# Products that need no corrected value, moved ahead of the waits in an RWKV-7 state phase

## The chip, the cores and the metric

The kernel runs on one core of a Trainium2 chip. The metric is the device time of one execution in microseconds. The core has five engines with a program each: PE (matrix products), DVE (vector), ACT (activation), POOL, and SP, which issues the DMAs. They meet only through semaphores. A product's result lies in one of eight PSUM banks until DVE or ACT has read it.

## The reference

A decoder trunk of two layers over 256 tokens of width 1024: an RWKV-7 time mix and a SwiGLU FFN, then dilated window attention and a second FFN. The change lies in the time mix, whose core is a recurrence of a 64 x 64 state for each of 16 heads, followed by a normalization of the output over each head:

```python
def step(state, inp):
    r_t, w_t, k_t, v_t, a_t, b_t = inp
    sa = jnp.einsum('bhij,bhj->bhi', state, a_t)
    state = (state * w_t[:, :, None, :] + sa[..., None] * b_t[:, :, None, :]
             + v_t[..., None] * k_t[:, :, None, :])
    return state, jnp.einsum('bhij,bhj->bhi', state, r_t)
...
o = wkv7_scan(rh, decay, kh, vh, -kk, kk * ah)
mean = jnp.mean(o, axis=-1, keepdims=True)
var = jnp.mean(jnp.square(o - mean), axis=-1, keepdims=True)
o = (o - mean) * lax.rsqrt(var + LNX_EPS)
```

## The kernel before

**Groups and chunks.** The time mix runs in four groups of 256 columns, that is four heads each (`it` 0 to 3), and each group in two chunks of 128 tokens. Within a chunk the recurrence is solved in closed form: masked products of scaled keys, receptances and values (the planes of `M`: 0 and 1 with the b vectors, 2 and 3 with the keys; 0 and 2 against a, 1 and 3 against r), a triangular inverse `Us` that is built over six levels, and from it the corrected values. The index `u` is a head of chunk 0 (0 to 3) or of chunk 1 (4 to 7).

**The tail of a group** (lines 805 to 849) is where the change lies. In the names of the code:

- `Zs`: what the values of earlier tokens and the carried state put on the a vectors. For chunk 0 there is no state; for chunk 1 it is `M` plane 2 by the values `Vn`, plus `ar` by the state `St` (bank 4, signalled as `pe_z1`).
- `UUs`: the corrected values, `Us` by `Zs` (banks 1 and 5, signalled as `pe_uu`, copied to SBUF by ACT, which signals `act_uu`).
- `St`: the state after chunk 0, keys by values (`kPn`, `Vn`) plus b by corrected values (`bPn`, `UUs`), in bank 2; DVE decays it and signals `dve_S`.
- The output of a chunk (banks 3 and 6, signalled as `pe_o`): `ar` by the state (chunk 1 only), `M` plane 3 by the values and `M` plane 1 by the corrected values.

**What stands between.** Each wait of PE on another engine in the tail is covered by `next_keys(v)`: in groups 0 to 2 a quarter of the next group's key projection, 12 products of 256 columns; in the last group, which has no successor, a few products of the identity with itself (`keep_clock`), whose result nobody reads.

**Behind the tail.** The output is normalized over each head (`norm_output`, lines 1645 to 1668, on DVE): sum, mean, centring (`dve_oc`), ACT's square (`square_output`), sum of squares (`dve_var`), POOL's inverse root, scaling (`dve_on`). Chunk 0 goes first, then chunk 1. On ACT the order is fixed by the program text (lines 1284 to 1296): copy of chunk 1's `Zs`, copy of chunk 1's corrected values, then, in groups 0 to 2, a sigmoid of one element, ahead of which a table load stands, then the square of chunk 0. In the next group PE projects three quarters of the receptances, transposes the normalized output (`turn_output`, line 596), sums the squares of the keys and goes on. In the last group ACT squares chunk 0 ahead of the two copies, and PE turns chunk 0's output between two waits of the tail, gates it (`gate_output` on DVE) and multiplies it by the output weights (`product_o`), then the same for chunk 1, which leads into the FFN.

All products of the tail are of fp32 operands; in the trace each such product stands as two records. The functions `mm` and `A` are helpers, so all products have line 496 and all of ACT's work line 1111.

Of the kernel before, what the change touches and what calls it, by code (L numbers as in the profile page):

```python
# [20 lines left out]
P = 128  # L21
D, T = 1024, 256
KT, RT = D // P, T // P
HD = 64
# [64 lines left out]
def program(nc, ins, out):  # L89
    ctx = ExitStack()  # L90
    with ctx:
# [3 lines left out]
        def sem(name):  # L95
            return ctx.enter_context(nc.semaphore(name))
# [59 lines left out]
        bank = [ctx.enter_context(nc.psum_tensor(f"bank{i}", [P, 512], F32)) for i in range(3)]  # L156
# [5 lines left out]
        bank = [b[:, :] for b in bank]  # L162
# [5 lines left out]
        def S(name):  # L168
            if name not in names:
                names[name] = sem(name)  # L170
            return names[name]
# [5 lines left out]
        M = work[:, 0:8 * 512].rearrange("p (u m t) -> p u m t", u=8, m=4)  # L177
# [18 lines left out]
        ar = cg.take(8 * P, "p (n c m t) -> p n c m t", n=2, c=2, m=2)  # L196
# [22 lines left out]
        Vn = spare_G.rearrange("p (c n i) -> p c n i", c=2, n=2)  # L219
        kPn, bPn = (spare_E[:, 256 * i:256 * i + 256].rearrange("p (n i) -> p n i", n=2) for i in range(2))  # L220
        Zs = cg.take(256)
        UUs = sa.rearrange("p n t -> p (n t)").rearrange("p (c n i) -> p c n i", c=2, n=2)
        St = cg.take(256, "p (n i) -> p n i", n=2)
# [270 lines left out]
        def _(pe):  # L494
            def mm(o, a, b, start=True, stop=True):
                return pe.matmul(o, a, b, start=start, stop=stop)  # L496

            def keep_clock(n, b):
                for _ in range(n):
                    mm(bank[b][:, 0:P], ident, ident)  # L500
# [25 lines left out]
            for k in range(KT):  # L526
                m = pe.transpose(bank[7][:, k * NR:(k + 1) * NR], rows[0:NR, k * P:(k + 1) * P], ident[0:NR, 0:NR])
            m.then_inc(S("pe_par"), 1)
            for r in range(RT):
                for j in range(2):  # L530
# [4 lines left out]
                    for q in range(4):  # L535
                        k = 4 * j + q
                        m = pe.transpose(bank[2 * r + j][:, q * P:(q + 1) * P], hn[:, r, k * P:(k + 1) * P], ident)
# [9 lines left out]
            for k in range(KT):  # L547
# [3 lines left out]
                if k % 4 == 3:  # L551
                    for s_ in range(4):
                        m = mm(bank[3 + s_][32 * s_:32 * s_ + 32, 0:T], g1s[:, k - 3 + s_, P:LG], xs[2][:, k - 3 + s_, :], k == 3, k == KT - 1)
# [26 lines left out]
            def project_parts(b, i, hi, parts, name, quarters=range(4)):  # L580

                w_parts = [v.rearrange("p (k n) -> p k n", k=KT) for v in (hi, mix_lo[:, i, :])]
                for n, k0 in ((v // 2, v % 2 * (KT // 2)) for v in quarters):
                    for k in range(k0, k0 + KT // 2):
                        for a, c in PASSES:
                            m = mm(bank[b][:, n * T:(n + 1) * T], w_parts[a][:, k, n * P:(n + 1) * P], parts[c][:, k, :],
                                   k == 0 and a + c == 0, k == KT - 1 and a == 1)
                if 3 in quarters:
                    m.then_inc(S(name), 1)
# [40 lines left out]
            def group(it, behind=True, ahead=True):  # L630


                def next_keys(v):
                    if ahead:
                        if v == 0:
                            pe.wait_ge(S("dve_x_lo"), 2)
                        if v < 2:
                            pe.wait_ge(S("dve_mix_lo"), it * 6 + v + 1)
                        project_parts(7, 1, kw_hi, (xk_hi, xk_lo), "pe_k", [v])
                    else:  # L640
                        keep_clock((4, 4, 4, 3)[v], 7)


                def sums_of_squares():
# [47 lines left out]
                for c in range(2):  # L692
# [5 lines left out]
                    for banks, src, read in ((MB, bP, 2), (MK, kP, 4)):  # L698
                        if c == 1:
                            pe.wait_ge(S("act_mats"), it * 8 + read)  # L700
                        for nn in range(2):
                            for h in range(2):
                                hp = slice(h * HD, (h + 1) * HD)
                                m = mm(bank[banks[h]][:, nn * 256:(nn + 1) * 256], src[hp, nn, c * P:(c + 1) * P],
                                       ar[hp, nn, c, :, :].rearrange("p m t -> p (m t)"))
# [47 lines left out]
                def quarter(b, u):  # L753
                    return b[:, u % 4 * QB:(u % 4 + 1) * QB]

                for l in range(1, LEVELS - 1):
                    corner = l == LEVELS - 2
                    for q in range(2):
# [3 lines left out]
                        for u in range(4 * q, 4 * q + 4):  # L762
                            for i, o in PAIRS if corner else zip(BLK, BLK):
                                w = corners[q][i, u % 4, o] if corner else M[i, u, 0, o]
                                m = mm(quarter(bank[q], u)[o, :], w, Tq[i, u, :])
# [6 lines left out]
                    for q in range(2):  # L772
                        pe.wait_ge(S("dve_X"), it * 12 + 2 * l + q - 1)
                        for u in range(4 * q, 4 * q + 4):
                            for o, i in PAIRS if corner else zip(BLK, BLK):
                                m = mm(quarter(bank[2 + q], u)[o, :], (Xq if corner else Xc)[i, u, :], Uc[i, u, :])
# [7 lines left out]
                for q in range(2):  # L784
                    pe.wait_ge(S("dve_U"), it * 12 + 11 + q)
                    for u in range(4 * q, 4 * q + 4):
                        m = pe.transpose(bank[4 + q][lo, u % 4 * HD:(u % 4 + 1) * HD], Us[lo, u, lo], ident[lo, lo])  # L787
                    m.then_inc(S("pe_T"), 1)
                next_keys(0)
                for q in range(2):  # L790
                    pe.wait_ge(S("act_T"), it * 2 + q + 1)
                    for u in range(4 * q, 4 * q + 4):
                        m = mm(bank[q][up, u % 4 * HD:(u % 4 + 1) * HD], corners[q][lo, u % 4, up], Tc[lo, u, :])
                    m.then_inc(S("pe_X"), 1)
                for q in range(2):
                    pe.wait_ge(S("dve_X"), it * 12 + 11 + q)
                    for u in range(4 * q, 4 * q + 4):
                        m = mm(bank[2 + q][lo, u % 4 * HD:(u % 4 + 1) * HD], Xc[up, u, :], Us[up, u, up])
                    m.then_inc(S("pe_U"), 1)

                def hcols(v, u):
                    return v[:, u * HD:(u + 1) * HD]
# [4 lines left out]
                for u in range(4):  # L807
                    m = mm(hcols(bank[1], u), Us[:, u, :], hcols(Zs, u))
                m.then_inc(S("pe_uu"), 1)
                next_keys(1)  # L810
                pe.wait_ge(S("act_uu"), it * 2 + 1)
                for n in range(2):
                    mm(bank[2][:, n * P:(n + 1) * P], kPn[:, n, :], Vn[:, 0, n, :], True, False)
                    m = mm(bank[2][:, n * P:(n + 1) * P], bPn[:, n, :], UUs[:, 0, n, :], False, True)
                m.then_inc(S("pe_S"), 1)
                for u in range(4):
                    hh = slice((u % 2) * HD, (u % 2 + 1) * HD)
                    mm(hcols(bank[3], u), M[:, u, 3, :], Vn[:, 0, u // 2, hh], True, False)
                    m = mm(hcols(bank[3], u), M[:, u, 1, :], UUs[:, 0, u // 2, hh], False, True)
                m.then_inc(S("pe_o"), 1)  # L820

                pe.wait_ge(S("dve_S"), it + 1)
                pe.wait_ge(S("pool_M"), it * 2 + 2)
                for n in range(2):
                    mm(bank[4][:, n * P:(n + 1) * P], ar[:, n, 1, 0, :], St[:, n, :], True, False)
                    for h in range(2):
                        u = 2 * n + h
                        m = mm(hcols(bank[4], u), M[:, 4 + u, 2, :], Vn[:, 1, n, h * HD:(h + 1) * HD], False, h == 1)
                m.then_inc(S("pe_z1"), 1)
                next_keys(2)  # L830
                pe.wait_ge(S("act_z"), it * 2 + 2)
                pe.wait_ge(S("act_U"), it * 2 + 2)
                for u in range(4):
                    m = mm(hcols(bank[5], u), Us[:, 4 + u, :], hcols(Zs, u))
# [2 lines left out]
                if not ahead:  # L837
                    turn_output(NGRP, [0])
                pe.wait_ge(S("act_uu"), it * 2 + 2)
                for n in range(2):  # L840
                    mm(bank[6][:, n * P:(n + 1) * P], ar[:, n, 1, 1, :], St[:, n, :], True, False)
                    for h in range(2):
                        u = 2 * n + h
                        hh = slice(h * HD, (h + 1) * HD)
                        o = hcols(bank[6], u)
                        mm(o, M[:, 4 + u, 3, :], Vn[:, 1, n, hh], False, False)
                        m = mm(o, M[:, 4 + u, 1, :], UUs[:, 1, n, hh], False, h == 1)
                m.then_inc(S("pe_o"), 1)


# [7 lines left out]
            project(7, 1, xk, "pe_k", (1, 2, 3))  # L858
            pe.wait_ge(s_const, 16)
            group(0, behind=False)  # L860
            for it in range(1, NGRP):
                group(it, ahead=it < NGRP - 1)
# [1334 lines left out]
```

## Time and profile before

| | |
|---|---|
| median of 3 runs | 928.52 us (928.47 to 928.74) |
| profiled execution | 934.33 us |
| span of its instructions | 932.0 us |
| mean granted clock of TensorE | 0.993 |
| PE busy / DVE / ACT / POOL | 920.8 / 681.7 / 501.8 / 101.4 us |

The four groups of the time mix lie in the span's first 263 us. The tail of group 0 runs from 75.6 to 88.0 us, those of groups 1 and 2 from 133.6 to 146.0 and from 190.8 to 203.2, that of the last group from 249.3 to 262.8. Times are from the start of the span. The granted clock is a share of 2.4 GHz.

### The profile page before, as it was taken

How to read it: one execution, taken by the hardware profiler on the slowest of the kernel's cores; microseconds unless marked ns; L12 is line 12 of the kernel's file. 1: busy time of each engine (PE TensorE's matmuls, PEld its weight loads, DVE VectorE, ACT ScalarE, POOL GpSimd, SP SyncE). 2: the span in 40 equal slices, each digit the busy share in tenths (PEclk: the TensorE clock that was granted, in tenths of full speed). 3: DMA queues.
4: the chain of work that ended last, by engine and by line, in shares of the span. 5: the costliest groups of instructions: out<-in, count | busy, mean ns of one | idle time of the engine just before them, and what ended most of it. 6: DMA issues, size and time to landing. Idle time of an engine off the chain costs nothing.

```text
span 932.0 us, 18317 instructions
## 1 busy us (share of the span) xinstructions
PE 920.8 (99%) x7008; PEld 818.6 (88%) x7008; DVE 681.7 (73%) x1294; ACT 501.8 (54%) x818; POOL 101.4 (11%) x75
## 2 busy tenths in 40 slices
PE   9999999999999999999999999999999999999998
PEld 7789889798879888888899999999998888888887
DVE  7877877778466756666687888889879666666665
ACT  4563544544244545444457776767777445445442
POOL 0211000000012000000041133213222000000000
PEclk9999999999799999999999999999999999999999
DMA  9311213203407676667369545554654256676661
GB/s 298 132 60 46 91 60 105 92 1 107 145 1 202 178 223 178 185 193 217 104 206 292 152 132 163 148 155 139 171 159 114 71 162 186 192 203 195 188 180 45
DMA packets 195241, 136.71 MB, mean 147 GB/s; under 512 B 7390, under 2 KB 186078, under 8 KB 195180
## 3 DMA queue, kind: packets, MB, share of 16 engines
q1 hardware_dynamic: 194748, 135.13, 49.3%
q8 instruction: 44, 0.72, 0.3%
q10 hardware_dynamic: 432, 0.72, 0.3%
q14 instruction: 17, 0.14, 0.1%
HBM read 134.78 MB, written 1.05 MB: 146 GB/s over the span
## 4 chain that ended last, share of the span: by engine, by line
PE 94%; DVE 3%; issue 2%; ACT 1%; POOL 0%; POOLq 0%; DVEq 0%
PE bank L496 52%; PE wide L496 37%; DVE work L1505 1%; PE wide L1029 1%; PE wide L1052 1%; PE bank L1029 1%; PE bank L1052 1%; DVE x L1505 0%; POOL gsm L2123 0%; PE wide L653 0%; PE wide L741 0%; PE wide L787 0%; PE bank L519 0%; ACT work L1111 0%; PE bank L596 0%
## 5 line engine op out<-in xcount | busy, mean ns | idle before, releaser
L496 PE MATMUL bank<-wpj,hkq 128*128 128x384 f32 x1152 | 215.5, 340 | 1.5 <-ACT Vs L1111 0.4
L496 PEld LDWEIGHTS bank<-wpj,hkq 128*128 128x128 f32 x1152 | 197.5, 188 | 6.1 <-issue 4.2
L496 PE MATMUL wide<-hsp,wsp 128*128 128x256 f32 (+2 forms) x1120 | 196.0, 329 | 1.6 <-DVE hsp L1505 1.6
L496 PEld LDWEIGHTS wide<-hsp,wsp 128*128 128x128 f32 x1120 | 172.4, 190 | 24.3 <-DVE hsp L1505 2.4
L1505 DVE TENSOR_TENSOR wsp<-ring,wsp 128x1024 fp32r<-128x1024 f32 (+1 forms) x88 | 150.6, 1752 | 4.2 <-ACT wsp L1111 4.2
L1111 ACT ACTIVATE wsp<-ring 128x1024 fp32r<-128x1024 f32 (+1 forms) x88 | 130.3, 1484 | 26.5 <-DMA ring<-in_f_w_gu 15.6
L2123 POOL TENSOR_TENSOR gsm<-gsm,mhalf 128x6 f32<-128x6 f32 (+1 forms) x40 | 74.3, 1876 | 317.4 <-DVE gsm L2041 174.0
L1111 ACT ACTIVATE rows<-wide 128x256 f32<-128x256 f32 x66 | 25.4, 384 | 145.7 <-PE wide L496 145.7
L496 PE MATMUL bank<-wsp,asp 128*128 128x512 f32 x396 | 98.1, 392 | 0.0
L1505 DVE TENSOR_TENSOR wpj<-ring,wpj 128x1536 fp32r<-128x1536 f32 x48 | 84.1, 1753 | 17.0 <-ACT wpj L1111 17.0
L496 PEld LDWEIGHTS bank<-wsp,asp 128*128 128x128 f32 x396 | 71.8, 189 | 13.1
L1111 ACT ACTIVATE wpj<-ring 128x1536 fp32r<-128x1536 f32 x48 | 71.1, 1485 | 6.6 <-PE bank L496 6.3
L496 PEld LDWEIGHTS bank<-work 64*64 64x64 f32 (+4 forms) x1216 | 58.9, 140 | 16.1 <-issue 6.2
L496 PE MATMUL bank<-work 64*64 64x32 f32 (+7 forms) x1216 | 71.1, 237 | 1.6
L1505 DVE TENSOR_TENSOR am<-sg,rows 128x256 f32<-128x256 f32 x44 | 19.1, 435 | 71.4 <-ACT sg L1111 70.8
L496 PE MATMUL bank<-hsp,wsp 128*128 128x256 f32 (+1 forms) x368 | 68.7, 330 | 0.0
L1111 ACT ACTIVATE work<-wide 128x256 f32<-128x256 f32 (+3 forms) x73 | 30.9, 441 | 67.6 <-PE wide L496 28.6
L496 PE MATMUL wide<-work 64*64 64x32 f32 (+6 forms) x720 | 62.7, 265 | 0.7 <-DVE work L1505 0.4
L496 PEld LDWEIGHTS bank<-hsp,wsp 128*128 128x128 f32 x368 | 56.9, 190 | 6.2
L496 PEld LDWEIGHTS wide<-work 64*64 64x64 f32 (+4 forms) x720 | 54.4, 160 | 4.5 <-issue 1.7
L1505 DVE TENSOR_TENSOR rows<-wide,rows 128x256 f32<-128x256 f32 x66 | 27.9, 424 | 37.3 <-ACT rows L1111 37.3
L496 PE MATMUL wide<-wsp,asp 128*128 128x512 f32 x132 | 37.1, 390 | 0.0
(295 smaller groups left out, 1333.4 us busy)
## 6 DMA issues: line engine op xcount, KB each, us to landing
ring<-in_f_w_gu SPq DMA_DIRECT2D x88, 512.0 KB, 6.0
ring<-in_w_kv SPq DMA_DIRECT2D x96, 256.0 KB, 3.5
ring<-in_f_w_down SPq DMA_DIRECT2D x44, 512.0 KB, 3.7
ring<-in_b_w_q SPq DMA_DIRECT2D x48, 256.0 KB, 3.4
wmix<-in_a_w_k SPq DMA_DIRECT2D x4, 1024.0 KB, 5.2
wmix<-in_a_w_r SPq DMA_DIRECT2D x4, 1024.0 KB, 5.6
wmix<-in_a_w_v SPq DMA_DIRECT2D x4, 1024.0 KB, 5.3
wmix<-in_a_w_o SPq DMA_DIRECT2D x4, 1024.0 KB, 5.0
```

Of the source, the lines that this page charges most:

```text
L496: return pe.matmul(o, a, b, start=start, stop=stop)
L1029: m = pe.transpose(QK[w][r][:, g * P:(g + 1) * P], akr[:, 2 * w + r, g * P:(g + 1) * P], ident)
L1052: m = pe.transpose(SCORES[r][h][:, j * P:(j + 1) * P], pr[r][:, h, j * P:(j + 1) * P], ident)
L1111: return act.activation(o, i, f, **k)
L1505: return dve.tensor_tensor(o, a, b, op)
L2123: return pool.tensor_tensor(dst, src, mhalf[:, 0:n], ALU.pow)
```

## The change

Only PE's program is edited. Four moves and a subtraction:

- Chunk 0's keys by values go from behind the wait for chunk 0's corrected values to a place ahead of it (ahead of `next_keys(1)`).
- Chunk 1's plane 2 by values go from behind the wait for the state to a place ahead of it; the wait for POOL's masks moves with them.
- Chunk 1's `ar` by state and plane 3 by values, which open its output, go from behind the wait for chunk 1's corrected values to a place right behind `pe_z1`, ahead of `next_keys(2)`.
- A bank's first product alone opens the accumulation and its last alone closes it.
- In the last group `keep_clock` does 4, 2, 3 and 3 products, not 4, 4, 4 and 3.

```diff
-                        keep_clock((4, 4, 4, 3)[v], 7)
+                        keep_clock((4, 2, 3, 3)[v], 7)
...
                 m.then_inc(S("pe_uu"), 1)
+                for n in range(2):
+                    mm(bank[2][:, n * P:(n + 1) * P], kPn[:, n, :], Vn[:, 0, n, :], n == 0, False)
                 next_keys(1)
                 pe.wait_ge(S("act_uu"), it * 2 + 1)
                 for n in range(2):
-                    mm(bank[2][:, n * P:(n + 1) * P], kPn[:, n, :], Vn[:, 0, n, :], True, False)
-                    m = mm(bank[2][:, n * P:(n + 1) * P], bPn[:, n, :], UUs[:, 0, n, :], False, True)
+                    m = mm(bank[2][:, n * P:(n + 1) * P], bPn[:, n, :], UUs[:, 0, n, :], False, n == 1)
                 m.then_inc(S("pe_S"), 1)
...
                 m.then_inc(S("pe_o"), 1)
+                pe.wait_ge(S("pool_M"), it * 2 + 2)
+                for u in range(4):
+                    mm(hcols(bank[4], u), M[:, 4 + u, 2, :], Vn[:, 1, u // 2, u % 2 * HD:(u % 2 + 1) * HD], u == 0, False)
 
                 pe.wait_ge(S("dve_S"), it + 1)
-                pe.wait_ge(S("pool_M"), it * 2 + 2)
                 for n in range(2):
-                    mm(bank[4][:, n * P:(n + 1) * P], ar[:, n, 1, 0, :], St[:, n, :], True, False)
-                    for h in range(2):
-                        u = 2 * n + h
-                        m = mm(hcols(bank[4], u), M[:, 4 + u, 2, :], Vn[:, 1, n, h * HD:(h + 1) * HD], False, h == 1)
+                    m = mm(bank[4][:, n * P:(n + 1) * P], ar[:, n, 1, 0, :], St[:, n, :], False, n == 1)
                 m.then_inc(S("pe_z1"), 1)
+                for n in range(2):
+                    mm(bank[6][:, n * P:(n + 1) * P], ar[:, n, 1, 1, :], St[:, n, :], n == 0, False)
+                for u in range(4):
+                    mm(hcols(bank[6], u), M[:, 4 + u, 3, :], Vn[:, 1, u // 2, u % 2 * HD:(u % 2 + 1) * HD], False, False)
                 next_keys(2)
...
                 pe.wait_ge(S("act_uu"), it * 2 + 2)
-                for n in range(2):
-                    mm(bank[6][:, n * P:(n + 1) * P], ar[:, n, 1, 1, :], St[:, n, :], True, False)
-                    for h in range(2):
-                        u = 2 * n + h
-                        hh = slice(h * HD, (h + 1) * HD)
-                        o = hcols(bank[6], u)
-                        mm(o, M[:, 4 + u, 3, :], Vn[:, 1, n, hh], False, False)
-                        m = mm(o, M[:, 4 + u, 1, :], UUs[:, 1, n, hh], False, h == 1)
+                for u in range(4):
+                    m = mm(hcols(bank[6], u), M[:, 4 + u, 1, :], UUs[:, 1, u // 2, u % 2 * HD:(u % 2 + 1) * HD], False, u == 3)
                 m.then_inc(S("pe_o"), 1)
```

What this does to PE's order is shown at two places. `wide` holds banks 3 and 4, `wide2` banks 5 and 6; the size behind an operation is partitions by columns of the moving operand. First group 0 (groups 1 and 2 read alike), from the wait for chunk 0's corrected values to the third quarter of the key projection. Before:

```order
L496 MATMUL bank2<-work 128x128 [waits act_uu]
L496 MATMUL bank2<-work 128x128 x3
L496 MATMUL wide<-work 128x64 x8
L496 MATMUL wide<-work 128x128 [waits pool_M,dve_S]
L496 MATMUL wide<-work 128x64 x2
L496 MATMUL wide<-work 128x128
L496 MATMUL wide<-work 128x64 x2
L496 MATMUL bank7<-x_hi,w_hi 128x256
```

And changed, the same stretch:

```order
L496 MATMUL bank2<-work 128x128 [waits act_uu]
L496 MATMUL bank2<-work 128x128
L496 MATMUL wide<-work 128x64 x8
L496 MATMUL wide<-work 128x64 [waits pool_M]
L496 MATMUL wide<-work 128x64 x3
L496 MATMUL wide<-work 128x128 [waits dve_S]
L496 MATMUL wide<-work 128x128
L496 MATMUL wide2<-work 128x128 x2
L496 MATMUL wide2<-work 128x64 x4
L496 MATMUL bank7<-x_hi,w_hi 128x256
```

Two keys-by-values products have left the top of the stretch, and the six products into `wide2` that open chunk 1's output now stand ahead of the key projection, which itself stands ahead of the corrected values of chunk 1.

Second the last group, from the wait for the state to the output of chunk 1 (`bank7<-cst` are the fillings, line 596 turns chunk 0's output). Before:

```order
L496 MATMUL wide<-work 128x128 [waits pool_M,dve_S]
L496 MATMUL wide<-work 128x64 x2
L496 MATMUL wide<-work 128x128
L496 MATMUL wide<-work 128x64 x2
L496 MATMUL bank7<-cst 128x128 x4
L496 MATMUL wide2<-work 128x64 [waits act_U,act_z]
L496 MATMUL wide2<-work 128x64 x3
L496 MATMUL bank7<-cst 128x128 x3
L596 MATMUL bank2<-cst,work 128x128 [waits dve_on]
L596 MATMUL bank2<-cst,work 128x128
L496 MATMUL wide2<-work 128x128 [waits act_uu]
L496 MATMUL wide2<-work 128x64 x4
```

And changed:

```order
L496 MATMUL wide<-work 128x128 [waits dve_S]
L496 MATMUL wide<-work 128x128
L496 MATMUL wide2<-work 128x128 x2
L496 MATMUL wide2<-work 128x64 x4
L496 MATMUL bank7<-cst 128x128 x3
L496 MATMUL wide2<-work 128x64 [waits act_U,act_z]
L496 MATMUL wide2<-work 128x64 x3
L496 MATMUL bank7<-cst 128x128 x3
L596 MATMUL bank2<-cst,work 128x128 [waits dve_on]
L596 MATMUL bank2<-cst,work 128x128
L496 MATMUL wide2<-work 128x64 [waits act_uu]
L496 MATMUL wide2<-work 128x64 x3
```

The six products into `wide2` moved up past the third fillings (one fewer), the corrected values, the fourth fillings and the transposes; of chunk 1's output only the four products by the corrected values stay behind the last wait.

## Rows read from the trace of the kernel before

**Rows 1.** The page, busy time of each engine: us (share), instructions.

```profile
PE 920.8 (99%) x7008; PEld 818.6 (88%) x7008; DVE 681.7 (73%) x1294; ACT 501.8 (54%) x818; POOL 101.4 (11%) x75
```

**Rows 2.** Chain of waits, 80 to 108 us: start, us, what.

```profile
83.59 0.85 PE wide L496 x8
...
84.46 0.39 ACT work L1111
...
84.87 1.28 ACT L1111
...
87.41 1.93 POOL gsm L2123
...
94.04 0.66 PE bank L596 x4
```

**Rows 3.** Timeline of PE, 72 to 100 us: start, us, operation [idle before].

```profile
83.43 1.00 PE L496 MATMUL wide<-work 128*128 128x64 f32 x8
84.23 0.37 PE L496 MATMUL bank<-x_hi,w_hi 128*128 128x256 f32 x1
...
85.73 2.34 PE L496 MATMUL wide<-work 128*128 128x128 f32 x20
88.00 1.14 PE L496 MATMUL bank<-work,wa 64*128 64x256 f32 x8
...
94.04 0.66 PE L596 MATMUL bank<-cst,work 128*128 128x128 f32 x4 [0.44 <-DVE work L1505]
```

**Rows 4.** Timeline of ACT, 72 to 100 us.

```profile
84.46 0.39 ACT L1111 ACTIVATE work<-wide 128x256 f32<-128x256 f32 x1 [1.92 <-PE wide L496]
```

**Rows 5.** Timeline of DVE, 72 to 100 us.

```profile
81.48 0.42 DVE L1505 TENSOR_TENSOR work<-wide,gsm 128x256 f32<-128x256 f32 x1
...
84.09 2.35 DVE L1505 TENSOR_TENSOR wmix_low<-wmix,vw_hi 128x1024 fp32r<-128x1024 f32 x2
...
93.59 0.39 DVE L1505 TENSOR_TENSOR work<-work,gsm 128x256 f32<-128x256 f32 x1
```

**Rows 6.** Timelines of PE and DVE at the second and third turn.

```profile
151.41 0.60 PE L596 MATMUL bank<-cst,work 128*128 128x128 f32 x4
...
150.66 0.39 DVE L1505 TENSOR_TENSOR work<-work,gsm 128x256 f32<-128x256 f32 x1
...
208.68 0.60 PE L596 MATMUL bank<-cst,work 128*128 128x128 f32 x4
...
207.93 0.39 DVE L1505 TENSOR_TENSOR work<-work,gsm 128x256 f32<-128x256 f32 x1
```

**Rows 7.** Timeline of PE and its weight loads (PEld), last group's tail.

```profile
251.03 2.02 PE L496 MATMUL bank<-cst 128*128 128x128 f32 x8
...
257.63 1.11 PE L496 MATMUL bank<-cst 128*128 128x128 f32 x8
258.58 1.00 PE L496 MATMUL wide<-work 128*128 128x64 f32 x8
...
260.29 0.20 PEld L596 LDWEIGHTS bank<-cst,work 128*128 128x128 f32 x2 [0.18 <-DVE work L1505]
...
262.75 3.65 PE L496 MATMUL bank<-wmix,work 128*128 128x512 f32 x8
```

**Rows 8.** Timeline of DVE in the last group's tail, 248 to 274 us.

```profile
261.41 0.42 DVE L1505 TENSOR_TENSOR work<-work 128x256 f32<-128x256 f32 x1
262.95 0.42 DVE L1653 TENSOR_REDUCE gsm<-wide 128x4 f32<-128x256 f32 x1 [1.11 <-PE wide L496]
```

**Rows 9.** Engines' busy time by stretch; PEclk is the granted clock's share.

```profile
70.30:73.60 3.30, 3.30 (x20) 3.08 (x20) 1.23 (x2) 0.28 (x2) 0.00 (x0) 0.50 0.00 0
240.00:244.00 4.00, 3.88 (x99) 3.37 (x95) 3.31 (x12) 2.59 (x7) 0.00 (x0) 1.00 0.03 10
244.40:254.50 10.10, 10.10 (x63) 9.76 (x63) 3.15 (x3) 1.26 (x4) 0.00 (x0) 0.50 0.26 74
...
249.30:254.50 5.20, 5.20 (x25) 5.20 (x25) 1.20 (x1) 0.76 (x2) 0.00 (x0) 0.50 0.50 144
```

## The prediction

> **What bounds the kernel now.** The page comes first: PE is busy 99% of the span [rows 1]. That share alone would say that only fewer PE instructions help. So the chain of waits is read next, round the end of the first column group, where the edit lies. There the chain leaves PE at 84.44, passes through ACT, DVE and POOL, and comes back at 94.04 with four transposes [rows 2]; in between PE works on other things, so it looks busy, but it isn't what is waited for. The timelines of the engines say what that detour is. The eight PE records at 83.43 are the corrected values of chunk 1 (four products; an fp32 product leaves two records) [rows 3]. ACT copies them at 84.46, having been idle 1.92 us for them [rows 4], and everything behind that copy on ACT is in program order: the table load (84.87, 1.28 us), the one-element sigmoid, and the square of chunk 0's centred output. DVE had that output centred from 81.48 on, 0.42 us long [rows 5], so the square could have begun some 2.5 us before the copy; it doesn't, because it stands behind it. From the square on: sum, POOL's root (87.41), the scaling, then the same for chunk 1, and at 93.59 DVE writes the scaled output that the transposes need. PE has no work left and idles 0.44 us ahead of them [rows 3]. At the second turn (group 1 to 2) and the third (2 to 3) the same write begins at 150.66 and 207.93, and PE comes to its transposes at 151.41 and 208.68 without a wait [rows 6].
>
> In these three tails PE waits for nothing: products follow at the spacing of back-to-back records from 83.43 through 88.00 [rows 3], because projections of the next group's keys stand in every wait. The last group has no next keys; there identity products fill, and PE (its weight load) waits once, 0.18 us, at 260.29 [rows 7].
>
> **The change, part by part.**
>
> *Groups 0 to 2.* The same products are issued, so PE's end of the tail doesn't move, unless a wait goes; there is none to take. What moves is the order. Four records (keys by values) go ahead of the key projection; PE reaches the state products no sooner, since the total ahead of them is equal: nothing. Eight records (values through the mask, chunk 1) go ahead of the wait for the state: nothing either, for the same reason. Twelve records of the chunk 1 output (4 of 128 columns, 8 of 64) move from behind the last wait to a place ahead of the third key projection, and so ahead of the corrected values of chunk 1. Those come later by the price of twelve records. Twenty such records start at 85.73 and the next work at 88.00 [rows 3]: 2.27 us, 0.1135 each, so 12 x 0.1135 = 1.36 us. The bounds: by the eight narrow ones at 83.43, 0.80 us to the next row [rows 3], 12 x 0.100 = 1.20; and as the twenty less eight narrow ones, 2.27 - 0.80 = 1.47.
>
> The copy on ACT, then the table load, the square and the whole detour move by this 1.36 us; no step of it has another input that comes later (DVE's low parts of the weights end at 84.09 + 2.35 = 86.44 [rows 5], ahead of the sum even now). At the first turn there is no slack, since PE waits already: +1.36. At the other two the write ends at 150.66 + 0.39 = 151.05 and 207.93 + 0.39 = 208.32; the hand-over takes 0.06 (93.59 + 0.39 = 93.98 to 94.04), so PE could have gone 0.30 earlier each time [rows 3, 5, 6]. 1.36 - 0.30 = +1.06 each. Sum: 1.36 + 1.06 + 1.06 = +3.48. Behind the transposes on PE stand the sums of squares of the keys, and for them wait ACT's root, the scaled keys and the triangular solve; nothing there has a source that doesn't move along, so I let all of it reach the end. The key weights that SP loads when the projection is done (chunk after chunk, used a group later) start 1.36 us later and are hidden by a whole solve.
>
> *The last group.* Here records are removed: two fillings in the wait for chunk 0's corrected values and one in the wait for chunk 1's state part, six records. Eight such cost 258.58 - 257.63 = 0.95 [rows 7], so 6 x 0.119 = 0.71. (The first two stand at half clock, where they cost nearly double, 2.02 us busy for eight at 251.03 against 1.11 for eight at 257.63 [rows 7]; but PE is busy throughout, and if the clock comes back at the same moment as now, what is saved ahead of it is that much work at full clock.) The 0.18 us wait at 260.29 also goes, since the twelve records now stand ahead of it: PE would be through with the chunk 1 output 0.89 earlier. Two things hold it. The transposes of chunk 0 were reached at 260.29 - 0.18 = 260.11; now 260.11 - 0.71 + 1.36 = 260.76, 0.47 later than they ran. DVE's gating behind them, which ended at 261.41 + 0.42 = 261.83, ends at 262.30, and the output product starts at 262.36 and not at 262.75 [rows 7, 8]: -0.39. DVE, which must finish that gating first, then begins the sums of chunk 1 at 262.30 and not at 262.95 [rows 8]: -0.65. This second chain decides, as the sums lead to the root, the next transposes and the FFN's input. I take -0.65, with -0.39 and -0.89 as bounds.
>
> **The sum**: 3.48 - 0.65 = +2.83 us. It is made on the profiled execution, which took 934.33 us (span 932.0 and 2.33 around it), 5.81 more than the median of 928.52. Applied to the median: 931.35, so **931.4**. Bounds of the terms alone: 1.20 + 0.90 + 0.90 - 0.89 = +2.1 and 1.47 + 1.17 + 1.17 - 0.39 = +3.4, so 930.6 to 931.9; as the slack at the second and third turn may be some tenths more in an execution without a profile, 930.4 to 931.9.
>
> **Rivals.**
>
> *The delay is hidden; not slower.* The 5.81 us by which the profiled execution is longer may lie in the detours of many small instructions, so that without a profile the scaled output is ready earlier against PE. Where it is ready 1.36 us ahead at each turn, nothing is lost and the last group's gain stands: 928.52 - 0.65 = 927.9. For it: I can't see where the 5.81 lies. Against it: at the first turn PE waits 0.44 now, and the detour would have to shrink by 1.8 of 9.6 us.
>
> *The half clock goes; not slower.* From 244.4 to 254.5 PE ran at the lower of its two levels (0.50, 1.2 GHz), and also from 70.3 to 73.6; the longer stretch began after 4 us in which PE was busy 3.88 us, with 99 small records [rows 9]. The change shifts the later groups by 1 to 3 us and could move them off the moment at which the clock falls. In 249.3 to 254.5, 25 records took 5.20 us, 0.208 each [rows 9], against 0.119 for a filling at full clock: 25 x 0.089 = 2.2 us is the least that a recovered stretch gives; half of 10.1, that is 5.0, the most. Middle 3.6: 931.4 - 3.6 = 927.8.
>
> *Another stretch at half clock; slower still.* The same shift could make the clock fall in group 1 or 2, where it now holds. A short stretch (3.3 us) costs at most 1.65, a long one the 3.6 above: 933.0 to 935.0. The Trainium skill (TensorE: Matmul & The Clock Gate, Part 1) ties the lower clock to an idle engine. The trace differs, as the busy 3.88 of 4 us just given show; by the page neither of these two rivals would have a chance, and the forecast would stand as it is.
>
> *The early products are cheap; not slower by a measurable amount.* If a 64-column record cost half of a 128-column one (0.119 from the fillings [rows 7]), twelve would take 4 x 0.119 + 8 x 0.059 = 0.95, the turns 0.95 + 0.65 + 0.65, and the sum would be +1.6: 930.1. Against it stands that eight narrow records took 0.80 us and eight wide fillings 0.95 [rows 3, 7]. The Trainium skill (the same page, Back-to-back issue gap) goes further: 60 cycles for up to 64 columns and 134 for 128. By that the twelve would take an estimated 0.42 us, and the whole change about nothing, 928.5. Its section on loading weights, by which the time goes with the 128 columns of the weights, agrees with the rows instead.
>
> **Chances.** Forecast 0.60; hidden 0.12; half clock gone 0.10; another half-clock stretch 0.13; cheap products 0.05. A change of 0.2% (1.9 us, about what a measurement of this kernel can tell from none) begins at 930.4 and 926.7. Slower: the forecast less 0.01 at its lower edge, and the further stretch, 0.72. Faster: the most favourable part of the recovered clock (a gain of 5.0 gives 926.4), 0.04. Same: 0.24. The range reaches from the hidden case to a short further stretch, 927.7 to 933.0; the likeliest case's own is 930.4 to 931.9.
>
> **What would show it.** In groups 0 to 2 of the changed kernel ACT's copy of the corrected values of chunk 1 should start some 1.36 us later, with a longer idle time ahead of it (1.92 becomes about 3.3), and PE should wait about 1.8, 1.06 and 1.06 us ahead of the transposes at the three turns. In the last group the output product should start about 0.4 and the second transposes about 0.65 us earlier, counted from the first corrected values. The granted clock should fall in the same two places. The forecast is wrong if PE doesn't wait at the second and third turn, or if the clock's stretches change in number.

## The result, and the profile after

| | before | changed |
|---|---|---|
| median of 10 | 929.07 us (928.47 to 931.48) | 933.22 us (931.28 to 936.72) |
| ratio, 95% interval | | 1.0042 [1.003, 1.0055] |
| profiled execution | 934.33 us, span 932.0 | 934.60 us, span 932.3 |

The change makes the kernel slower by 0.42%, 3.9 us. The ten times of the changed kernel fall in two parts by their mean granted clock: five executions at 1.000 take 931.28 to 932.18 us, five at 0.995 or 0.996 take 934.26 to 936.72. The median, 933.22, is the middle between the two parts; no execution lies there. The profiled one belongs to the second part. The profiled execution of before had a clock of 0.993; other executions of that kernel at 1.000 have spans of 925.8 us and up. So the two spans, 932.0 and 932.3, must not be compared as they stand; stages are compared instead.

Chain of waits of the changed kernel, 82 to 97 us, the lines that answer to [rows 2]:

```profile
83.89 0.85 PE wide L496 x8
...
84.76 0.38 ACT work L1109
...
85.16 1.28 ACT L1109
...
87.71 1.93 POOL gsm L2121
...
94.35 0.66 PE bank L596 x4
```

It is the same detour as before, from the corrected values of chunk 1 through ACT's copy to the transposes, and of the same length: 83.89 to 94.35 is 10.46, 83.59 to 94.04 was 10.45. What has changed is where it starts. PE's timeline round it, 75 to 100 us (answers to [rows 3]):

```profile
77.82 4.58 PE L496 MATMUL wide<-work 128*128 128x64 f32 x40
...
83.72 1.00 PE L496 MATMUL wide<-work 128*128 128x64 f32 x8
...
86.05 1.00 PE L496 MATMUL wide<-work 128*128 128x64 f32 x8
86.98 1.13 PE L496 MATMUL bank<-work,wa 64*128 64x256 f32 x8
...
94.35 0.66 PE L596 MATMUL bank<-cst,work 128*128 128x128 f32 x4 [1.77 <-DVE work L1503]
```

Of the 40 records at 77.82 the last twelve open chunk 1's output; behind the corrected values (83.72) only eight are left for it (86.05). From the corrected values to the next group's first product, PE needed 88.00 - 83.43 = 4.57 us and now needs 86.98 - 83.72 = 3.26: it gets there 1.31 us sooner after the corrected values, while the detour takes as long as ever. So it waits 1.77 us at the transposes where it waited 0.44. ACT's timeline shows the other side of it (answers to [rows 4]):

```profile
84.76 0.38 ACT L1109 ACTIVATE work<-wide 128x256 f32<-128x256 f32 x1 [3.23 <-PE wide L496]
```

The copy of chunk 1's corrected values now follows 3.23 us of idleness, not 1.92. PE at the second and third turn (answers to [rows 6]):

```profile
155.55 0.66 PE L596 MATMUL bank<-cst,work 128*128 128x128 f32 x4 [0.86 <-DVE work L1503]
...
213.88 0.66 PE L596 MATMUL bank<-cst,work 128*128 128x128 f32 x4 [0.87 <-DVE work L1503]
```

Before, neither of these turns had a wait [rows 6]. The last group (PE answers to [rows 7]):

```profile
259.53 0.89 PE L496 MATMUL bank<-cst 128*128 128x128 f32 x6
260.25 1.00 PE L496 MATMUL wide<-work 128*128 128x64 f32 x8
261.09 0.89 PE L496 MATMUL bank<-cst 128*128 128x128 f32 x6
261.81 0.38 PE L596 MATMUL bank<-cst,work 128*128 128x128 f32 x2
262.03 1.00 PE L496 MATMUL wide<-work 128*128 128x64 f32 x8
263.36 3.70 PE L496 MATMUL bank<-wmix,work 128*128 128x512 f32 x8 [0.32 <-DVE work L1503]
```

No wait is left ahead of the transposes of chunk 0 (261.81), and the output product (263.36) now waits 0.32 us for DVE's gating of chunk 0, as the prediction had it. The engines' busy time by stretch, with the granted clock as PEclk (answers to [rows 9]):

```profile
92.50:94.30 1.80, 0.08 (x1) 0.00 (x0) 1.72 (x6) 1.80 (x7) 1.02 (x1) 1.00 0.00 0
95.10:101.90 6.80, 6.80 (x33) 6.80 (x33) 4.44 (x11) 4.20 (x7) 0.00 (x0) 0.50 0.21 68
102.00:110.00 8.00, 8.00 (x62) 7.15 (x61) 6.20 (x12) 1.98 (x5) 0.00 (x0) 1.00 0.49 160
```

PE is busy 0.08 of the 1.80 us ahead of the transposes, and from 95.1 to 101.9 it runs at the lower level (1.2 GHz), on projections whose records come at 0.21 us each. In this execution the stretches of before at 70 and 244 us are absent. So the clock's stretches changed in number, from two to one, which the prediction had named as a sign of being wrong.

### The profile page after: what moved, and what is told of

It reads as the page before. It is cut to its first block, busy times and chain, and to the rows that moved or that the text cites. A ratio compares the mean times of both kernels' runs of the same rounds, so it can differ in the third digit from the quotient of the medians.

```text
span 932.3 us, 18301 instructions
## 1 busy us (share of the span) xinstructions
PE 917.8 (98%) x7002; PEld 815.4 (87%) x7002; DVE 681.4 (73%) x1294; ACT 501.3 (54%) x818; POOL 101.2 (11%) x75
## 3 DMA queue, kind: packets, MB, share of 16 engines
HBM read 134.78 MB, written 1.05 MB: 146 GB/s over the span
## 4 chain that ended last, share of the span: by engine, by line
PE 92%; DVE 4%; issue 2%; ACT 1%; POOL 0%; POOLq 0%; DVEq 0%
PE bank L496 51%; PE wide L496 37%; DVE work L1503 2%; PE bank L1050 1%; PE wide L1027 1%; PE bank L1027 1%; PE wide L1050 1%; ACT work L1109 0%; DVE work L1698 0%; POOL gsm L2121 0%; ACT L1109 0%; DVE x L1503 0%; PE wide L741 0%; PE wide L653 0%; PE wide L787 0%
## 5 line engine op out<-in xcount | busy, mean ns | idle before, releaser
L496 PE MATMUL bank<-work 64*64 64x32 f32 (+7 forms) x1216 | 68.3, 233 | 1.8
L496 PEld LDWEIGHTS bank<-work 64*64 64x64 f32 (+4 forms) x1216 | 55.8, 135 | 16.2 <-issue 5.9
```

## The experiments

Two theories were on record for the delay. **A**: it runs through ACT's order, the late copy holding up the table load and the square of chunk 0. **B**: the products cost more where they stand now. For the executions at a lower clock there were **C**, the wait at the first turn lets the clock fall, and **D**, the shift of the groups does.

**square_first** (the changed kernel, ACT's order edited):

```diff
-                    if c == 1 and not ahead:
-                        square_output(NGRP, 0)
+                    if c == 1:
+                        square_output(it + 1, 0)
...
                     A(small[:, 63:64], onec[:, 0:1], ACT.Sigmoid)
-                    square_output(it + 1, 0)
```

> The changed kernel, but in groups 0 to 2 ACT squares chunk 0's centred output ahead of the two copies of chunk 1, as it does in the last group already. PE's program is that of the change. Theory A (the delay runs through ACT's order: late copy, then table load and square): chunk 0's normalization no longer hangs on the corrected values of chunk 1, so the extra waits at the three turns go, PE waits under 0.4 us ahead of the transposes at the first turn and not at the others, and only the last group's gain is left: 927.3 to 928.2 us at full clock. Theory B (the products themselves cost more where they stand now, or open the accumulation at a price): nothing moves, 931.3 at full clock as the changed kernel.

Measured: 927.74 us, ratio to before 0.9979 [0.9966, 0.9992]; none of 12 executions is under a clock of 0.998. ACT's timeline at the first turn:

```profile
80.22 0.42 ACT L1109 ACTIVATE work<-work 128x256 f32<-128x256 f32 x1 [2.89 <-DVE work L1502]
80.55 0.37 ACT L1109 ACTIVATE work<-wide 128x256 f32<-128x256 f32 x1
84.09 0.39 ACT L1109 ACTIVATE work<-wide 128x256 f32<-128x256 f32 x1 [3.18 <-PE wide L496]
```

And PE's:

```profile
83.06 1.00 PE L496 MATMUL wide<-work 128*128 128x64 f32 x8
85.36 1.00 PE L496 MATMUL wide<-work 128*128 128x64 f32 x8
...
91.98 0.65 PE L596 MATMUL bank<-cst,work 128*128 128x128 f32 x4
```

The square (80.22) now precedes the copy of the corrected values by 3.9 us. That copy is as late as in the changed kernel (idle 3.18 us ahead of it). PE's program is unedited, and its row at the transposes shows no wait. Theory A holds, B falls: the products cost no more where they stand now than where they stood.

**open_late_in_013** (the six products wait again for the last corrected values in groups 0, 1 and 2, label notwithstanding; in the last group, which isn't `ahead`, they stay early):

```diff
-                for n in range(2):
-                    mm(bank[6][:, n * P:(n + 1) * P], ar[:, n, 1, 1, :], St[:, n, :], n == 0, False)
-                for u in range(4):
-                    mm(hcols(bank[6], u), M[:, 4 + u, 3, :], Vn[:, 1, u // 2, u % 2 * HD:(u % 2 + 1) * HD], False, False)
+                def open_output():
+                    for n in range(2):
+                        mm(bank[6][:, n * P:(n + 1) * P], ar[:, n, 1, 1, :], St[:, n, :], n == 0, False)
+                    for u in range(4):
+                        mm(hcols(bank[6], u), M[:, 4 + u, 3, :], Vn[:, 1, u // 2, u % 2 * HD:(u % 2 + 1) * HD], False, False)
+
+                if not ahead:
+                    open_output()
                 next_keys(2)
...
                 pe.wait_ge(S("act_uu"), it * 2 + 2)
+                if ahead:
+                    open_output()
```

> The changed kernel, but the six products that open chunk 1's output stand ahead of the third key projection in the last group alone; in groups 0 to 2 they are back behind the wait for the corrected values. Theory A: ACT's copy of the corrected values comes at the time of before (idle 1.9 us ahead of it), no waits at the second and third turn, 0.4 at the first, and the last group keeps its 0.65: 927.9 us at full clock. If the last group gains nothing: 928.5. Theory B (the moves of keys by values and of plane 2 cost as well): over 929.

Measured: 928.38 us, ratio 0.999 [0.9977, 1.0004]; the median of its six executions at clock 1.000 is 927.84, that of 23 of before beside it 929.15. PE at the three turns:

```profile
93.20 0.66 PE L596 MATMUL bank<-cst,work 128*128 128x128 f32 x4 [0.44 <-DVE work L1509]
...
150.50 0.60 PE L596 MATMUL bank<-cst,work 128*128 128x128 f32 x4
...
207.68 0.60 PE L596 MATMUL bank<-cst,work 128*128 128x128 f32 x4
...
260.81 0.38 PE L596 MATMUL wide<-cst,work 128*128 128x128 f32 x2
```

The first turn's wait is that of before to the hundredth, the others are gone. From the third turn to the transposes of chunk 1 (207.68 to 260.81) it takes 53.13 us.

**open_late_all** (the third move undone in all groups; the first two and the three fillings given up stay: the six products follow `pe.wait_ge(S("act_uu"), it * 2 + 2)` everywhere).

> The changed kernel with the third move undone in all four groups; the first two moves and the three fillings given up stay. Theory A: turns as before, and the last group gains only by the first two fillings, since its wait for chunk 0's scaled output is still there: 928.5 - 0.44 = 928.1 us at full clock. Theory B: the first two moves cost part of the 2.8, over 929.

Measured: 928.52 us, ratio 0.9986 [0.997, 1.0003]. PE's rows:

```profile
92.48 0.65 PE L596 MATMUL bank<-cst,work 128*128 128x128 f32 x4 [0.45 <-DVE work L1503]
...
207.03 0.60 PE L596 MATMUL bank<-cst,work 128*128 128x128 f32 x4
```

Counted from the first record of chunk 0's corrected values to the transposes, the three turns take 18.45, 17.83 and 17.84 us, and 18.45, 17.84 and 17.85 in before: the first two moves cost nothing there. The time itself can't tell a gain of 0.4 us from none.

**open_early_alone** (the kernel before with the third move alone; the six products stand behind `pe_z1` and leave the last wait, as in the change's diff).

> The kernel before with the third move alone (the six products that open chunk 1's output, in all four groups); the first two moves aren't made and the fillings are 4, 4, 4 and 3. Theory A: the turns cost 1.36 + 1.05 + 1.03 = 3.44, and the last group gains nothing, as chunk 0's gating comes 1.2 us later and DVE begins the sums of chunk 1 at the same time (+0.07): 932.0 us at full clock, more where the clock falls in the wait at the first turn. Theory B: 928.5 to 929.

Measured: 935.31 us, ratio 1.0068 [1.0049, 1.0087]. One execution of six is at 1.000 (931.94), five at 0.995 or 0.996 (934.87 to 937.14). PE:

```profile
93.81 0.66 PE L596 MATMUL bank<-cst,work 128*128 128x128 f32 x4 [1.78 <-DVE work L1503]
...
152.16 0.66 PE L596 MATMUL bank<-cst,work 128*128 128x128 f32 x4 [0.89 <-DVE work L1503]
...
210.55 0.66 PE L596 MATMUL bank<-cst,work 128*128 128x128 f32 x4 [0.89 <-DVE work L1503]
```

The third move by itself makes all three waits of the changed kernel. Its loss at full clock rests on that one execution: 931.94, where 932.0 was expected, is 2.8 above the 929.15 of before beside it.

**open_late_in_0** (as open_late_in_013, with `it > 0` for `not ahead` and `it == 0` for `ahead`).

> The changed kernel with the third move undone in group 0 alone. Theory A, with a price for each turn of its own: the first turn's 1.36 us is given back, the second and third keep 1.05 and 1.03, the last group its gain: 931.35 - 1.36 = 930.0 us at full clock. Theory C: PE waits 0.44 us at the first turn as before, and no execution falls to half clock there. If the delay of one turn were swallowed by the next: 931.3 or 927.9.

Measured: 931.48 us, ratio 1.0024 [1.0014, 1.0033]; four executions of 11 at 1.000, median 930.38, lowest 929.71, and before beside it 928.72 and 928.04. PE waits 0.44, 0.86 and 0.88 us at the three turns. The loss at full clock, 1.66 to 1.67, is nearer to 1.05 + 1.03 - 0.65 = 1.43 than to 2.8 or to a gain: the turns add up singly, none swallows another's delay. The profiled execution is at 1.000; where the clock fell in the seven below it (0.994 to 0.999) isn't known. Of the 31 of before beside it 14 are below 1.000 too, so this run says little on C.

**square_first_on_before** (ACT's edit on the kernel before) and **both_repairs** (ACT's edit and open_late_in_013).

> The kernel before with ACT's square of chunk 0 ahead of the copies of chunk 1, and nothing else. Theory A: at the first turn the chain then waits for DVE's low parts of the weights and not for the square, 0.25 us sooner; at the second and third PE didn't wait: 928.5 - 0.25 = 928.25 us. If square_first owes its gain to ACT's order alone and not to the last group: 927.5.

> Third move in the last group alone, and ACT squares chunk 0 ahead of the copies of chunk 1 in all groups. Theory A: the square moved ahead already hides the delay of the third move, so taking that move back in groups 0 to 2 adds nothing: the same as square_first within 0.3 us, 927.3 to 927.6 at full clock. If part of the delay was still there in square_first, up to 1 us less.

Measured: 928.25 us, 0.9991 [0.9979, 1.0003], and 928.77 us, 0.9994 [0.9985, 1.0003]. At 1.000 their medians are 928.01 (of 7) and 927.56 (of 5). Neither is told from before by its interval; the order at full clock is the expected one, and both_repairs isn't better than square_first (927.63 of 10, on another chip). square_first_on_before has the last group of before at full clock, which the first profile lacked: from the third turn to the transposes of chunk 1 it takes 262.70 - 208.94 = 53.76 us. Its PE rows from the third turn on:

```profile
208.94 0.60 PE L596 MATMUL bank<-cst,work 128*128 128x128 f32 x4
...
247.76 1.08 PE L496 MATMUL bank<-work 128*128 128x64 f32 x8
...
258.70 3.65 PE L496 MATMUL bank<-wmix,work 128*128 128x512 f32 x8
...
262.70 0.44 PE L596 MATMUL wide<-cst,work 128*128 128x128 f32 x2
```

Against 53.13 in open_late_in_013 that is a gain of 0.63 for the last group; open_late_all, with the fillings alone, takes 260.40 - 207.03 = 53.37, a gain of 0.39. The same shows in the changed kernel itself, counted from the first corrected values as the prediction asked (rows of the changed kernel):

```profile
252.81 1.58 PE L496 MATMUL bank<-work 128*128 128x64 f32 x12
...
267.12 0.38 PE L596 MATMUL wide<-cst,work 128*128 128x128 f32 x2
```

To the output product (263.36) it takes 10.55 us, and 258.70 - 247.76 = 10.94 in square_first_on_before: 0.39 earlier. To the second transposes it takes 14.31, and 262.70 - 247.76 = 14.94 there: 0.63 earlier.

**fill_the_turns**, **changed_again** and **fill_first_turn** are for the clock. The first and third are the changed kernel with identity products ahead of the transposes at the turns (7, 3 and 3, and 7 at the first alone); the second is the changed kernel itself beside the third.

```diff
                     project_parts(4, 0, rw_hi, (xr_hi, xr_lo), "pe_r", (0, 1, 2))
+                    keep_clock((0, 7, 0, 0)[it], 5)
                     turn_output(it)
```

> The changed kernel, with identity products ahead of the transposes at the turns: 7 at the first, 3 each at the second and third, so that PE works where it now waits. They lie inside the waits (7 x 2 records x 0.117 = 1.64 of 1.77 us; 0.70 of 0.86), so at full clock nothing is lost: 931.3 to 931.6. Theory C (the clock falls because of the wait of 1.77 us at the first turn): no execution has the half-clock stretch behind the first turn that the changed kernel's profile shows at 95 us, and the times near 934.4 are gone. Theory D (it falls by the shift of the solves against the moments at which the clock can change): executions near 934.4 remain in a like share, 5 of 10.

> The changed kernel unaltered, beside the next one on the same chip. If the wait of 1.77 us at the first turn is what lets the clock fall (theory C), about half of the executions have a mean granted clock of 0.995 or 0.996 and take some 934.5 us, the others 931.3 to 932.2 at 1.000, as in the first ten.

> The changed kernel with 7 identity products ahead of the transposes at the first turn alone. Theory C: no execution at 0.995 or 0.996; those without a fall elsewhere take 931.3 to 932.2. Theory D (the falls come from the shift of the groups, not from that wait): the same share near 934.5 as in the unaltered kernel beside it.

Measured: fill_the_turns 932.21 us, 1.0048 [1.0028, 1.0067], with clocks of 0.998 to 1.000 and one of 0.993 (939.70) in 8 executions; the four at 1.000 take 931.92 to 932.08, some 0.5 us above what was expected, though the second and third turn take 18.88 us each, as in the changed kernel. changed_again 934.45 us, 1.0063 [1.0049, 1.0077], all five at 0.995 or 0.996, where about half was expected. fill_first_turn 932.01 us, 1.0033 [1.0021, 1.0044], six of seven at 1.000 (931.79 to 932.51) and one at 0.996 (934.27), where theory C expected none. In changed_again's profile the busy time by stretch is

```profile
70.60:73.90 3.30, 3.30 (x19) 3.08 (x19) 1.27 (x2) 0.32 (x2) 0.00 (x0) 0.50 0.00 0
93.50:95.70 2.20, 0.44 (x4) 0.23 (x2) 2.06 (x8) 2.20 (x8) 1.02 (x1) 1.00 0.00 0
97.90:101.20 3.30, 3.30 (x18) 3.30 (x17) 3.23 (x9) 2.83 (x5) 0.00 (x0) 0.50 0.15 47
```

and in fill_first_turn's, round the same turn:

```profile
88.00:94.00 6.00, 5.85 (x50) 5.66 (x49) 4.36 (x15) 2.86 (x9) 2.39 (x2) 1.00 0.43 141
94.00:102.00 8.00, 7.91 (x66) 7.69 (x66) 7.07 (x18) 5.03 (x9) 0.00 (x0) 1.00 0.41 132
```

With the wait filled the clock holds in six of seven executions; open, on the same chip, it holds in none of five. Over all runs, of 21 executions with an open wait of 1.8 us at the first turn 15 have a clock of 0.996 or less and the others 1.000; of 85 of the other edited kernels 7 have 0.996 or less, and 20 more 0.998. So the wait lets the clock fall (C). How much of the second part's time it makes isn't shown: a mean clock doesn't say where the clock fell, only two of the 15 were profiled, and in one of these, changed_again, half of the time at half clock (70.6 to 73.9) lies ahead of the turn, in a stretch that before has as well [rows 9]. D isn't excluded for such stretches, which came without the wait.

## Why the prediction held, and where it was short

**The detour through ACT's order**: right. The twelve records delay the copy by 1.31 us (3.23 less 1.92), forecast 1.36 with bounds of 1.20 and 1.47. The waits of 1.77, 0.86 and 0.87 us compare with a forecast of 1.8, 1.06 and 1.06. The two later ones look 0.2 short, but a wait is counted from the modelled end of the product ahead of it. Counted from start to start, from the first of PE's records for the corrected values of chunk 0 to the transposes, there is nothing short. The starts in before,

```profile
75.59 1.08 PE L496 MATMUL bank<-work 128*128 128x64 f32 x8
...
133.57 1.08 PE L496 MATMUL bank<-work 128*128 128x64 f32 x8
...
190.83 1.08 PE L496 MATMUL bank<-work 128*128 128x64 f32 x8
```

and changed:

```profile
74.54 1.58 PE L496 MATMUL bank<-work 128*128 128x64 f32 x12
...
136.66 1.58 PE L496 MATMUL bank<-work 128*128 128x64 f32 x12
...
195.00 1.58 PE L496 MATMUL bank<-work 128*128 128x64 f32 x12
```

The first turn takes 94.35 - 74.54 = 19.81 us where before took 94.04 - 75.59 = 18.45, 1.36 later. The second takes 155.55 - 136.66 = 18.89 us where before took 151.41 - 133.57 = 17.84, and the third 213.88 - 195.00 = 18.88 against 208.68 - 190.83 = 17.85: 1.05 and 1.03 later. square_first shows the cause itself: the same late copy, no wait.

**Slack at the second and third turn**, 0.30 us: right within what the trace resolves.

**No price for the first two moves**: right, by open_late_all.

**The last group**, -0.65 with bounds of -0.39 and -0.89: right. It measured -0.63, in the changed kernel and in open_late_in_013 against square_first_on_before, and -0.39 for the fillings alone, where -0.44 was expected. That DVE's gating of chunk 0 limits it shows in the 0.32 us wait of the output product.

**The sum**, +2.8 us: the rows give 1.36 + 1.05 + 1.03 - 0.63 = 2.81. At full clock the changed kernel takes 931.3 to 932.2 and fill_first_turn 931.8 to 932.5, which is a median 2.9 above the 929.11 of before beside it. In the forecast's own case, 930.4 to 931.9, lie four of the first ten executions, and a fifth at 932.18.

**The clock**: here the prediction was short. The measured median, 933.22, lies 0.2 above the range's end, since half of the executions are the rival "another stretch at half clock", priced at 933.0 to 935.0 (one of the five is above that, at 936.72) and given a chance of 0.13. Before had a median of 929.07 this time and not 928.52; by the ratio 1.0042 the forecast's base gives 932.4, inside the range. That the middle comes out near the range's end is luck: with one more execution in the second part it is 934.3, and in changed_again it was 934.45.

The step that failed is the reason I gave for that rival: I let the clock fall by a shift of the solves' small products, and so took the wait of 1.8 us at the first turn, which the same prediction had worked out, for 1.36 us of delay and nothing else. The runs show that it can also let the clock fall: open, five of five executions are at 0.995 or 0.996, filled, one of seven. I had set the Trainium skill's tie to idleness (TensorE: Matmul & The Clock Gate, Part 1) against the stretch at 244 us, which came with PE busy 3.88 of 4 us [rows 9], and wrote that by the page the rival would have no chance. I did not ask what the idle 1.8 us that the forecast itself brings would do. Both kinds of fall occur here, one with PE busy on small products, one behind an idle 1.8 us. Nor does the busy kind come each time: in the changed kernel's profile PE is busy 3.88 of 4 us from 66.2 to 70.2, and the clock holds.

**The 5.81 us between profiled execution and median**, which I couldn't place: the profiled execution of before ran 13.7 us at half clock (70.24 to 73.65 and 244.32 to 254.56) and others ran at 1.000. Beside square_first the five executions of before at 0.993 take 933.99 to 934.49 and those at 1.000 have a median of 929.15. So it is in the main the clock, not the detours, and the rival "the delay is hidden" had no ground.

**The rival of cheap narrow products** fell: twelve records delayed the copy by 1.31 us, 0.109 each.

## What to carry to other kernels

A product moved ahead of a wait isn't free where the wait is already covered: it delays what stands behind it in its engine's order. Before filling a gap, follow what the next result releases on the other engines, and look there for work that stands behind it in program order without needing it; here PE's reordering alone lost (1.0042), the move of one square of 0.4 us on ACT alone can't be told from nothing (0.9991 [0.9979, 1.0003]), and the two together beat the kernel before (0.9979 [0.9966, 0.9992]). A wait of PE can have two prices, its length and what it does to the granted clock behind it; compare executions of equal mean clock before adding up terms.

## What the runs showed of the hardware that was not expected

The lower clock can cost more than the work that the wait holds up: the profiled execution of the changed kernel, whose only stretch at half clock (95.1 to 101.9) follows the first turn, takes 934.60 us, some 3 us above those at 1.000 (four of them 931.3 to 931.6), with a delay of 1.36 us at that turn. The fall came 0.7 us after PE had resumed in one profile (94.35 to 95.1, half clock to 101.9) and 2.2 us after in another (95.72 to 97.9), in neither during the wait. Seven identity products (1.72 us of PE) ahead of the transposes kept the clock in six of seven executions and delayed nothing at that turn: from the first corrected values to the transposes it takes 94.09 - 74.29 = 19.80 us with them and 19.81 without.
